# Layer 1's attention: two weight splits at its end instead of its start, and the compressed softmax's second half one turn later

## The chip, the cores and the metric

One core of a Trainium2 chip runs the whole program. TensorE (PE) multiplies, VectorE (DVE) and ScalarE (ACT) do elementwise work, GpSimd (POOL) scales the probabilities, and SyncE (SP) issues the weight loads. The metric is the device time of one execution, in microseconds (us), as the median of the executions timed; lower is better.

## The reference, cut to what matters

Two blocks follow each other; the change lies in layer 1 of the first. That layer's mixer has 16 heads in 4 groups of four and 256 queries, and adds up three attentions of each head: over 15 compressed keys, over selected keys and over a window. With 4 blocks of 64 keys all of them selected, and a window of 512 over 256 positions, the last two are plain causal attentions over different keys.

```python
s_c = jnp.einsum('bqgjd,bngd->bgjqn', qp, k_cmp).astype(jnp.float32) * scale
p_c = masked_softmax(s_c, cmp_end[None, :] <= qpos[:, None])
o_c = jnp.einsum('bgjqn,bngd->bqgjd', p_c.astype(v_cmp.dtype), v_cmp)
...
o = gc[..., 0:1] * o_c + gc[..., 1:2] * o_s + gc[..., 2:3] * o_w
...
return o.reshape(B, S, C_MIX_WIDTH) @ w_out
```

`masked_softmax` zeroes the masked places after the exponential and divides by the sum, at least 1e-20. A compressed key ends at position 31 or later, so the first 31 queries see none of them and get zeros. After the mixer come a product with `w_out` (1024 x 1024), the memory attention and the feed-forward.

## The kernel before

**Weights.** A weight matrix is cut into units of 128 x 2048 numbers (4 chunks of 128 rows by 512 columns). SP loads a unit into one of three slots `raw`; ACT writes its rounded copy `whi` (line 794, `hi`); DVE writes the rest, `wlo = raw - whi` (line 1250, `lo`); PE does three matmuls a chunk, with `whi`, `wlo` and `whi` (lines 2055 to 2057). A unit's load waits for the `lo` of the unit three before it, and its `hi` waits for the product that used that slot. Each engine has its own program, written out in order, and counts up semaphores for the others. `split_to(end)` splits the units up to `end` where it stands in ACT's program and in DVE's. The mixer's output product (`s["out"]`) has four units, here O0 to O3: O0 and O1 make the first 512 columns, O2 and O3 the second.

**The attention loop.** `attention` runs over 32 items (a head and a half of the queries, selected and window branch together), two of them a turn, `t = 0, 2, ..., 36`. In turn t, PE computes the scores of items t and t+1 (line 2146), which waits until DVE has masked the items before them; then runs `between(t)`; transposes the probabilities of items t-4 and t-3 (line 2156); and multiplies those of t-6 and t-5 with the values (lines 2163 and 2171, "PV" below). DVE takes the sums' reciprocals (1398, 1401), masks the scores with the causal bias and takes each row's minimum (1409), copies item t-4's transposed probabilities out of PSUM (1418), runs `between(t)` and `between(t+1)`, and every fourth turn writes a quarter of the product's input (`alo`, 1426). ACT takes exponentials (861), copies item t-3's transposed probabilities (871), runs `between(t)` and writes `ahi` (877). The last two turns only transpose and multiply; the output product begins as soon as PE has done the last PV. Turns alternate between scores 128 and 256 columns wide.

**The compressed softmax.** Its scores lie in four PSUM banks, two for each half `c` of the queries. Before the loop DVE adds the bias (1797), takes the maximum (1803) and subtracts it (1804), for both halves one after the other; ACT takes the exponentials (1133). In turns 0 and 2 of the loop (`compressed(1)` and `compressed(3)`) DVE multiplies a half by the mask `cmp_keep` (1815), sums (1816), bounds the sum from below (1817), inverts, multiplies by the gate and normalises (1818 to 1821). PE transposes both halves in turn 2 (2378); ACT copies the first, and DVE the second (1349), at the end of its turn 2. DVE and ACT split O0 in turn 6 and O1 in turn 10; O2 and O3 come after the loop.

Of the kernel before, what the change touches and what calls it, by code (L numbers as in the profile page):

```python
# [52 lines left out]
TINY = 1e-20  # L53
# [179 lines left out]
def build(nc, a, out):  # L233
    ctx = ExitStack()
    with ctx:
# [30 lines left out]
        cmp_bias, cmp_keep = sb("cmp_bias", [P, C, 32]), sb("cmp_keep", [P, C, 32])  # L266
# [423 lines left out]
        def _(pool):  # L690
# [15 lines left out]
            for c in range(C):  # L706
                step(pool.affine_select(out=cmp_keep[:, c, :], in_=cmp_keep[:, c, :], compare_op=ALU.is_ge, fill=0.0,
                                        base=P * c - (CMP_LEN - 1), pattern=[[-CMP_STRIDE, 32]], channel_multiplier=1))
# [77 lines left out]
        def _(act):  # L786
# [263 lines left out]
            for l in range(2):  # L1050
# [48 lines left out]
                else:  # L1099
# [31 lines left out]
                    for c in range(C):  # L1131
                        act.wait_ge(flag("cmp_shifted"), c + 1)
                        act.activation(CP[c], CS[c], ACT.Exp).then_inc(flag("cmp_exp"), 1)

                    def compressed(t):

                        if t == 0:
                            for b in range(2):
                                turn_copy(s["qrturn2"] + b, feat[:, 3072 + 512 * b:3584 + 512 * b])
                        if t == 2:  # L1140
                            turn_copy(s["cmpturn"], CPT[0])
                        if t in (6, 10):
                            split_to(s["vg"][-1].end + (t - 2) // 4)
# [100 lines left out]
        def _(dve):  # L1244
# [145 lines left out]
            def attention(items, run, banks, apart=False, between=None):  # L1390

                n, per = run.n, run.per
                for t in range(0, n + 6, 2):
                    for i in (t, t + 1):
# [8 lines left out]
                        if i < n:  # L1403
# [7 lines left out]
                            ins.then_inc(item_masked, 1)  # L1411
                    if 0 <= t - 4 < n:
# [244 lines left out]
            for l in range(2):  # L1657
# [88 lines left out]
                else:  # L1746
# [45 lines left out]
                    for c in range(C):  # L1792
# [14 lines left out]

                    def compressed(t):

                        if t in (1, 3):  # L1810
                            c = t // 2
                            cp4 = by_head(CP[c])
                            keep = cmp_keep[:, c, :].unsqueeze(1).broadcast_to([P, 16, 32])
                            dve.wait_ge(flag("cmp_exp"), c + 1)
                            step(dve.tensor_tensor(cp4, cp4, keep, ALU.mult))
                            step(dve.tensor_reduce(s_t[:, 0:16], cp4, AX, ALU.add))
                            step(dve.tensor_scalar(s_t[:, 0:16], s_t[:, 0:16], TINY, None, ALU.max))
                            step(dve.reciprocal(s_u[:, 0:16], s_t[:, 0:16]))
                            gate = GATE[:, c, :].rearrange("p (h b) -> p h b", b=3)[:, :, 0]
                            step(dve.tensor_tensor(s_u[:, 0:16], s_u[:, 0:16], gate, ALU.mult))  # L1820
                            dve.tensor_tensor(cp4, cp4, s_u[:, 0:16].unsqueeze(2).broadcast_to([P, 16, 32]), ALU.mult
                                              ).then_inc(flag("cmp_prob"), 1)
                        if t == 3:
                            turns(s["cmpturn2"], 1, lambda b: CPT[1])
                        if t in (6, 10):
                            split_to(s["vg"][-1].end + (t - 2) // 4)

                    attention(items1(), s["heads"], (2, 3, 0, 1), True, between=compressed)
# [223 lines left out]
        def _(pe):  # L2052
# [222 lines left out]
            for l in range(2):  # L2275
# [30 lines left out]
                else:  # L2306
# [61 lines left out]
                    def compressed(t):  # L2368
# [4 lines left out]
                        if t == 2:  # L2373
                            for c in range(C):
                                pe.wait_ge(flag("cmp_prob"), c + 1)
                                bank = turn_free(s["cmpturn"] + c)
                                for g in range(4):
                                    ins = pe.transpose(bank[:, P * g:P * g + P], CP[c][:, P * g:P * g + P], ident[:, :])
                                ins.then_inc(turned, 1)
# [240 lines left out]
```

## Time and profile before

| | |
|---|---|
| time, median of 3 runs | 1529.01 us (1528.53 to 1535.76) |
| the profiled execution: its time, its span | 1528.64 us, 1526.9 us |
| PE busy, of the span | 1371.0 us, 90% |
| DVE busy | 1053.4 us, 69% |
| ACT busy | 753.8 us, 49% |
| granted TensorE clock, mean of the span | 0.951 of full speed |

The span is what the trace covers; the time has 1.7 us more around it. Busy shares are means over the whole program. The loop of this change takes from 544 to 621 us of it, where the shares are others.

### The profile page before, as it was taken

How to read it: one execution, taken by the hardware profiler on the slowest of the kernel's cores; microseconds unless marked ns; L12 is line 12 of the kernel's file. 1: busy time of each engine (PE TensorE's matmuls, PEld its weight loads, DVE VectorE, ACT ScalarE, POOL GpSimd, SP SyncE). 2: the span in 40 equal slices, each digit the busy share in tenths (PEclk: the TensorE clock that was granted, in tenths of full speed). 3: DMA queues.
4: the chain of work that ended last, by engine and by line, in shares of the span. 5: the costliest groups of instructions: out<-in, count | busy, mean ns of one | idle time of the engine just before them, and what ended most of it. 6: DMA issues, size and time to landing. Idle time of an engine off the chain costs nothing.

```text
span 1526.9 us, 18368 instructions
## 1 busy us (share of the span) xinstructions
PE 1371.0 (90%) x6769; PEld 1130.9 (74%) x6769; DVE 1053.4 (69%) x1685; ACT 753.8 (49%) x943; POOL 110.1 (7%) x206
## 2 busy tenths in 40 slices
PE   6779698999998978889999998978789999999995
PEld 4667477788877856777888777867678787878784
DVE  4785766655554776676555478776567979888895
ACT  4343544444434446345444342553356757576773
POOL 0000301000000325120000000600000000000000
PEclk9989699999999979999999999999789999999997
DMA  6444024565546400234556634436548988989790
GB/s 226 141 164 138 15 70 138 166 192 191 176 157 164 137 18 32 64 128 159 188 192 192 186 126 150 162 114 212 207 151 302 337 323 313 346 283 354 284 348 28
DMA packets 123511, 277.63 MB, mean 182 GB/s; under 512 B 15383, under 2 KB 68781, under 8 KB 108077
## 3 DMA queue, kind: packets, MB, share of 16 engines
q1 hardware_dynamic: 121168, 275.99, 52.7%
q8 instruction: 46, 0.75, 0.2%
q10 hardware_dynamic: 2268, 0.65, 0.2%
q14 instruction: 29, 0.23, 0.0%
HBM read 275.57 MB, written 1.05 MB: 181 GB/s over the span
## 4 chain that ended last, share of the span: by engine, by line
PE 76%; DVE 15%; ACT 6%; issue 3%; ACTq 0%; POOL 0%; DVEq 0%
PE bank L2055 22%; PE bank L2057 21%; PE bank L2056 21%; PE bank L2490 2%; DVE t_wlo L1250 2%; DVE t_wlo L1261 2%; ACT t_whi L807 1%; PE bank L2156 1%; PE bank L2129 1%; PE bank L2146 1%; ACT t_whi L794 1%; DVE t_z L1409 1%; PE bank L2120 1%; PE bank L2171 1%; PE bank L2235 1%
## 5 line engine op out<-in xcount | busy, mean ns | idle before, releaser
L1250 DVE TENSOR_TENSOR t_wlo<-t_raw,t_whi 128x2048 fp32r<-128x2048 f32 (+3 forms) x144 | 316.6, 2209 | 151.2 <-ACT t_whi L794 150.0
L2055 PE MATMUL bank<-t_whi,t_ahi 128*128 128x512 f32 (+3 forms) x832 | 330.7, 397 | 31.2 <-DVE t_wlo L1250 13.2
L794 ACT ACTIVATE t_whi<-t_raw 128x2048 fp32r<-128x2048 f32 (+3 forms) x144 | 263.4, 1840 | 145.9 <-PE bank L2057 129.7
L2055 PE MATMUL bank<-t_whi,t_bhi 128*128 128x512 f32 (+1 forms) x800 | 314.3, 393 | 21.6 <-DVE t_z L1944 6.5
L2056 PE MATMUL bank<-t_wlo,t_ahi 128*128 128x512 f32 (+3 forms) x832 | 325.2, 391 | 0.0
L2057 PE MATMUL bank<-t_whi,t_alo 128*128 128x512 f32 (+3 forms) x832 | 325.1, 391 | 0.0
L2057 PE MATMUL bank<-t_whi,t_blo 128*128 128x512 f32 (+1 forms) x800 | 308.0, 385 | 0.0
L2056 PE MATMUL bank<-t_wlo,t_bhi 128*128 128x512 f32 (+1 forms) x800 | 307.7, 385 | 0.0
L2055 PEld LDWEIGHTS bank<-t_whi,t_ahi 128*128 128x128 f32 x832 | 159.4, 192 | 70.2 <-issue 28.3
L2055 PEld LDWEIGHTS bank<-t_whi,t_bhi 128*128 128x128 f32 x800 | 152.5, 191 | 53.6 <-issue 19.1
L2057 PEld LDWEIGHTS bank<-t_whi,t_alo 128*128 128x128 f32 x832 | 159.1, 191 | 32.2
L2056 PEld LDWEIGHTS bank<-t_wlo,t_ahi 128*128 128x128 f32 x832 | 159.4, 192 | 30.3
L2057 PEld LDWEIGHTS bank<-t_whi,t_blo 128*128 128x128 f32 x800 | 152.1, 190 | 30.5
L2056 PEld LDWEIGHTS bank<-t_wlo,t_bhi 128*128 128x128 f32 x800 | 152.6, 191 | 28.0
L1261 DVE TENSOR_TENSOR t_wlo<-t_raw,t_whi 128x2048 fp32r<-128x2048 f32 x51 | 116.2, 2288 | 26.4 <-ACT t_whi L807 26.1
L807 ACT ACTIVATE t_whi<-t_raw 128x2048 fp32r<-128x2048 f32 x51 | 97.9, 1920 | 40.4 <-PE bank L2057 40.3
L1261 DVE TENSOR_TENSOR t_wlo<-t_memo,t_whi 128x2048 fp32r<-128x2048 f32 x35 | 79.8, 2288 | 23.5 <-ACT t_whi L807 23.3
L807 ACT ACTIVATE t_whi<-t_memo 128x2048 fp32r<-128x2048 f32 x35 | 67.1, 1919 | 29.8 <-PE bank L2057 27.0
L1261 DVE TENSOR_TENSOR t_wlo<-t_feat,t_whi 128x2048 fp32r<-128x2048 f32 x34 | 77.6, 2287 | 4.9 <-ACT t_whi L807 4.7
L807 ACT ACTIVATE t_whi<-t_feat 128x2048 fp32r<-128x2048 f32 x34 | 65.2, 1919 | 25.3 <-PE bank L2057 25.1
L910 ACT ACTIVATE t_shared<-bank,t_half_scale 128x256 f32<-128x256 f32 x44 | 18.4, 470 | 76.8 <-PE bank L2057 73.5
L825 ACT ACTIVATE t_bhi<-bank,t_cols 128x256 fp32r<-128x256 f32 x40 | 15.7, 474 | 67.8 <-PE bank L2120 67.8
(370 smaller groups left out, 1421.7 us busy)
## 6 DMA issues: line engine op xcount, KB each, us to landing
t_raw<-in_ffn_w_in SPq DMA_DIRECT2D x88, 512.0 KB, 4.7
t_raw<-in_ffn_w_out SPq DMA_DIRECT2D x22, 1024.0 KB, 4.9
t_raw<-in_w_in SPq DMA_DIRECT2D x18, 1024.0 KB, 5.1
t_raw<-in_exp_w_up SPq DMA_DIRECT2D x18, 1024.0 KB, 6.9
t_raw<-in_exp_w_down SPq DMA_DIRECT2D x18, 1024.0 KB, 6.7
t_raw<-in_exp_w_gate SPq DMA_DIRECT2D x15, 1024.0 KB, 6.5
t_memo<-in_exp_w_gate SPq DMA_DIRECT2D x13, 1024.0 KB, 7.0
t_feat<-in_exp_w_up SPq DMA_DIRECT2D x13, 1024.0 KB, 7.1
```

The lines of the kernel that those rows point to most:

```text
L794: act.activation(whi[slot][:, 0:n], raw[slot][:, 0:n], ACT.Copy).then_inc(hi_done, 1)
L807: act.activation(whi[u % RING][:, :], RAW[slot], ACT.Copy).then_inc(hi_done, 1)
L825: ins = act.activation(dst[:, k, :], bank[:, T * n:T * n + T], ACT.Copy, scale=gain(k) if callable(gain) else gain)
L910: act.activation(silu[:, c, 0, :], TB[c][:, 0:FB], ACT.Tanh, scale=half_scale[:, c:c + 1]).then_inc(ff_tanh, 1)
L1250: dve.tensor_tensor(wlo[slot][:, 0:n], raw[slot][:, 0:n], whi[slot][:, 0:n].bitcast(F32), ALU.subtract).then_inc(lo_done, 1)
L1261: dve.tensor_tensor(wlo[u % RING][:, :], RAW[plan.raw_slot(u)], whi[u % RING][:, :].bitcast(F32), ALU.subtract).then_inc(lo_done, 1)
L1409: ins = dve.tensor_tensor_reduce(run.masked[g % 2][:, s_], SCB[g % 2][:, s_], b_.bias, -it.scale, -TAKEN, ALU.add, ALU.min, item_min[:, 2 ...
L2055: pe.matmul(dst, lhi, rhi_, start=start, stop=False)
L2056: pe.matmul(dst, lhi, rlo_, start=False, stop=False)
L2057: return pe.matmul(dst, llo, rhi_, start=False, stop=stop)
L2120: ins = pe.transpose(bank[:, T * n + P * c:T * n + P * c + P], src(c, 2 * b + n), ident[:, :])
L2490: ins = pe.matmul(y_bank(g, k // 4)[:, P * (k % 4):P * (k % 4) + P], x[:, c, k:D:KC], PICK[g % 2][:, c, :], start=c == 0, stop=c == 1)
```

## The change

Four edits, all in layer 1's attention:

1. O0 and O1 are split in turns 32 and 34 of the loop instead of turns 6 and 10, on ACT and DVE alike.
2. The second half's bias, maximum and subtraction move on DVE from ahead of the loop into turn 0, behind the masks of items 0 and 1; ACT's exponential of it moves into turn 0 too.
3. PE transposes the second half in turn 4 instead of turn 2, and DVE copies it in turn 4, ahead of item 0's copy (the new argument `ahead`).
4. The product with the mask and the lower bound of the sum go. `cmp_keep` shrinks to one number a row (0 for the 31 rows that see no compressed key, else 1), which goes in with the gate's product. The masked places carry a bias of -1e30 already, so their exponentials are zero wherever a row has a key.

```diff
-                    for c in range(C):
+                    def compressed_exp(c):
                         act.wait_ge(flag("cmp_shifted"), c + 1)
                         act.activation(CP[c], CS[c], ACT.Exp).then_inc(flag("cmp_exp"), 1)
+                    compressed_exp(0)
                     def compressed(t):
                         if t == 0:
+                            compressed_exp(1)
                             for b in range(2):
                                 turn_copy(s["qrturn2"] + b, feat[:, 3072 + 512 * b:3584 + 512 * b])
                         if t == 2:
                             turn_copy(s["cmpturn"], CPT[0])
-                        if t in (6, 10):
-                            split_to(s["vg"][-1].end + (t - 2) // 4)
+                        if t in (32, 34):
+                            split_to(s["vg"][-1].end + (t - 30) // 2)
...
+                    if ahead:
+                        ahead(t)
                     if 0 <= t - 4 < n:
                         i = t - 4
                         dve.wait_ge(turned, run.batch + i + 1)
...
+                    def compressed_prob(c):
+                        cp4 = by_head(CP[c])
+                        dve.wait_ge(flag("cmp_exp"), c + 1)
+                        step(dve.tensor_reduce(s_t[:, 0:16], cp4, AX, ALU.add))
+                        step(dve.reciprocal(s_u[:, 0:16], s_t[:, 0:16]))
+                        gate = GATE[:, c, :].rearrange("p (h b) -> p h b", b=3)[:, :, 0]
+                        step(dve.scalar_tensor_tensor(out=s_u[:, 0:16], in0=s_u[:, 0:16], scalar=cmp_keep[:, c, 0:1], in1=gate,
+                                                      op0=ALU.mult, op1=ALU.mult))
+                        dve.tensor_tensor(cp4, cp4, s_u[:, 0:16].unsqueeze(2).broadcast_to([P, 16, 32]), ALU.mult
+                                          ).then_inc(flag("cmp_prob"), 1)
+                    compressed_max(0)
                     def compressed(t):
+                        if t == 0:
+                            compressed_max(1)
                         if t in (1, 3):
-                            c = t // 2
-                            cp4 = by_head(CP[c])
-                            keep = cmp_keep[:, c, :].unsqueeze(1).broadcast_to([P, 16, 32])
-                            dve.wait_ge(flag("cmp_exp"), c + 1)
-                            step(dve.tensor_tensor(cp4, cp4, keep, ALU.mult))
-                            step(dve.tensor_reduce(s_t[:, 0:16], cp4, AX, ALU.add))
-                            step(dve.tensor_scalar(s_t[:, 0:16], s_t[:, 0:16], TINY, None, ALU.max))
...
-                        if t == 3:
-                            turns(s["cmpturn2"], 1, lambda b: CPT[1])
-                        if t in (6, 10):
-                            split_to(s["vg"][-1].end + (t - 2) // 4)
+                            compressed_prob(t // 2)
+                        if t in (33, 35):
+                            split_to(s["vg"][-1].end + (t - 31) // 2)
+                    def second_turn(t):
+                        if t == 4:
+                            turns(s["cmpturn2"], 1, lambda b: CPT[1])
...
-                        if t == 2:
-                            for c in range(C):
-                                pe.wait_ge(flag("cmp_prob"), c + 1)
...
+                        if t in (2, 4):
+                            c = t // 2 - 1
+                            pe.wait_ge(flag("cmp_prob"), c + 1)
```

**The start of the loop on DVE.** In the kernel before, from the second half's bias to the end of the first half's normalisation (the `ISA` rows are the masks of items 0 and 1; six more of them are left out):

```order
L1797 SCALAR_TENSOR_TENSOR t_shared<-bank,t_cmp_bias 128x128 x4
L1803 TENSOR_REDUCE t_s_t<-t_shared 128x16
L1804 TENSOR_TENSOR t_shared<-t_shared,t_s_t 128x512
L1409 ISA t_z,t_item_min<-bank,t_causal 128x128
L1409 ISA t_item_min 128x1
...
L1815 TENSOR_TENSOR t_z<-t_z,t_cmp_keep 128x512
L1816 TENSOR_REDUCE t_s_t<-t_z 128x16
L1817 TENSOR_SCALAR t_s_t<-t_s_t 128x16
L1818 RECIPROCAL t_s_u<-t_s_t 128x16
L1820 TENSOR_TENSOR t_s_u<-t_s_u,t_z 128x16
L1821 TENSOR_TENSOR t_z<-t_z,t_s_u 128x512
```

and in the changed kernel the same stretch:

```order
L1412 ISA t_z,t_item_min<-bank,t_causal 128x128
L1412 ISA t_item_min 128x1
...
L1803 SCALAR_TENSOR_TENSOR t_shared<-bank,t_cmp_bias 128x128 x4
L1809 TENSOR_REDUCE t_s_t<-t_shared 128x16
L1810 TENSOR_TENSOR t_shared<-t_shared,t_s_t 128x512
L1818 TENSOR_REDUCE t_s_t<-t_z 128x16
L1819 RECIPROCAL t_s_u<-t_s_t 128x16
L1821 SCALAR_TENSOR_TENSOR t_s_u<-t_s_u,t_cmp_keep,t_z 128x16
L1823 TENSOR_TENSOR t_z<-t_z,t_s_u 128x512
```

The masks of items 0 and 1 now stand ahead of the second half's three steps, and two of the six steps behind them are gone.

**The start of the loop on PE.** In the kernel before, from the scores of items 2 and 3 (256 wide) on; `t_ident<-t_z` rows are transposes of the compressed probabilities, `t_ident,t_feat` those of items 0 and 1:

```order
L2146 MATMUL bank<-t_feat 128x256 x2
L2146 MATMUL bank<-t_z,t_feat 128x256 x2
L2378 MATMUL bank<-t_ident,t_z 128x128 x8
L2146 MATMUL bank<-t_feat 128x128 x2
L2146 MATMUL bank<-t_z,t_feat 128x128 x2
L2156 MATMUL bank<-t_ident,t_feat 128x128 x4
```

and in the changed kernel:

```order
L2160 MATMUL bank<-t_feat 128x256 x2
L2160 MATMUL bank<-t_z,t_feat 128x256 x2
L2392 MATMUL bank<-t_ident,t_z 128x128 x4
L2160 MATMUL bank<-t_feat 128x128 x2
L2160 MATMUL bank<-t_z,t_feat 128x128 x2
L2392 MATMUL bank<-t_ident,t_z 128x128 x4
L2170 MATMUL bank<-t_ident,t_feat 128x128 x4
```

The scores of items 4 and 5 have moved ahead of the second half's transposes.

**The end of the loop on DVE.** In the kernel before, from the last reciprocals to O2's and O3's splits (`t_wlo`):

```order
L1398 RECIPROCAL t_item_inv<-t_item_sum 128x2
L1401 TENSOR_TENSOR t_item_inv<-t_item_inv,t_z 128x2
L1418 COPY t_shared<-bank 128x256
L1418 COPY t_shared<-bank 128x512
L1426 TENSOR_TENSOR t_alo<-bank,t_ahi 128x2x256
L1250 TENSOR_TENSOR t_wlo<-t_raw,t_whi 128x2048 x2
```

and in the changed kernel:

```order
L1401 RECIPROCAL t_item_inv<-t_item_sum 128x2
L1404 TENSOR_TENSOR t_item_inv<-t_item_inv,t_z 128x2
L1423 COPY t_shared<-bank 128x256
L1253 TENSOR_TENSOR t_wlo<-t_raw,t_whi 128x2048
L1423 COPY t_shared<-bank 128x512
L1253 TENSOR_TENSOR t_wlo<-t_raw,t_whi 128x2048
L1431 TENSOR_TENSOR t_alo<-bank,t_ahi 128x2x256
L1253 TENSOR_TENSOR t_wlo<-t_raw,t_whi 128x2048 x2
```

O0's split now stands between the copies of items 28 and 30, and O1's between the copy of item 30 and the last `alo`; on ACT the two `hi` stand behind the copies of items 29 and 31 in the same way.

## Rows read from the trace of the kernel before

**Rows 1.** Busy time and granted clock (PEclk) of seven stretches

```profile
core 0: us, PE busy (x) PEld busy (x) DVE busy (x) ACT busy (x) POOL busy (x), PEclk, DMA share, GB/s
161.00:183.00 22.00, 15.97 (x88) 11.19 (x90) 19.31 (x91) 9.25 (x37) 8.01 (x18) 0.51 0.01 2
279.00:286.00 7.00, 4.56 (x23) 3.49 (x22) 6.11 (x8) 5.05 (x5) 0.00 (x0) 1.00 0.51 150
547.00:556.00 9.00, 3.65 (x14) 2.35 (x15) 8.07 (x33) 5.68 (x20) 1.51 (x4) 0.50 0.00 0
556.00:571.00 15.00, 10.86 (x76) 7.85 (x74) 9.21 (x39) 6.93 (x22) 4.68 (x10) 0.70 0.02 1
621.00:650.00 29.00, 28.08 (x149) 23.86 (x147) 19.40 (x35) 12.64 (x19) 0.00 (x0) 1.00 0.28 87
917.00:920.00 3.00, 0.47 (x5) 0.50 (x6) 2.43 (x2) 0.00 (x0) 0.00 (x0) 1.00 0.13 38
920.00:923.50 3.50, 3.50 (x13) 2.93 (x12) 2.96 (x6) 0.00 (x0) 0.00 (x0) 0.51 0.85 292
```

**Rows 2.** Timeline of PE in the loop: start, duration, line, tiles, idle before

```profile
555.54 1.12 PE L2378 MATMUL bank<-t_ident,t_z 128*128 128x128 f32 x4 [3.66 <-DVE t_z L1821]
...
559.54 1.23 PE L2146 MATMUL bank<-t_feat 64*128 64x256 f32 x4 [0.67 <-DVE t_item_min L1409]
...
564.92 0.51 PE L2146 MATMUL bank<-t_feat 64*128 64x128 f32 x4
...
571.30 0.75 PE L2146 MATMUL bank<-t_feat 64*128 64x256 f32 x4 [3.50 <-DVE t_item_min L1409]
...
582.18 1.22 PE L2146 MATMUL bank<-t_feat 64*128 64x256 f32 x4 [3.54 <-DVE t_item_min L1409]
...
586.62 0.49 PE L2146 MATMUL bank<-t_feat 64*128 64x128 f32 x4
...
599.79 0.49 PE L2146 MATMUL bank<-t_feat 64*128 64x128 f32 x4 [0.80 <-DVE t_item_min L1409]
```

**Rows 3.** Timeline of DVE in turns 0 to 6 of the loop

```profile
544.79 0.88 DVE L1797 SCALAR_TENSOR_TENSOR t_shared<-bank,t_cmp_bias 128x128 f32<-128x128 f32 x4
...
547.03 0.28 DVE L1409 CUSTOM_DVE_ANT_0 t_z<-bank,t_causal 128x128 f32<-128x128 f32 x1
...
547.87 0.69 DVE L1815 TENSOR_TENSOR t_z<-t_z,t_cmp_keep 128x512 f32<-128x512 f32 x1
...
549.31 0.17 DVE L1817 TENSOR_SCALAR t_s_t<-t_s_t 128x16 f32<-128x16 f32 x1
...
550.63 0.16 DVE L1398 RECIPROCAL t_item_inv<-t_item_sum 128x2 f32<-128x2 f32 x1
...
552.55 0.78 DVE L1815 TENSOR_TENSOR t_z<-t_z,t_cmp_keep 128x512 f32<-128x512 f32 x1
...
556.70 0.69 DVE L1349 COPY t_shared<-bank 128x512 f32<-128x512 f32 x1 [1.21 <-PE bank L2378]
...
567.56 2.29 DVE L1250 TENSOR_TENSOR t_wlo<-t_raw,t_whi 128x2048 fp32r<-128x2048 f32 x1 [1.77 <-ACT t_whi L794]
```

**Rows 4.** Timeline of ACT: O0's `hi`, turn 32's copy, O3's `hi`

```profile
565.62 1.90 ACT L794 ACTIVATE t_whi<-t_raw 128x2048 fp32r<-128x2048 f32 x1
...
616.48 0.38 ACT L871 ACTIVATE t_shared<-bank 128x256 f32<-128x256 f32 x1 [1.88 <-PE bank L2171]
...
626.90 1.92 ACT L794 ACTIVATE t_whi<-t_raw 128x2048 fp32r<-128x2048 f32 x1 [2.37 <-PE bank L2057]
```

**Rows 5.** Timeline of the loop's end: DVE's last copy, PE's last PV, the output product

```profile
618.99 0.69 DVE L1418 COPY t_shared<-bank 128x512 f32<-128x512 f32 x1 [2.12 <-PE bank L2171]
...
619.83 0.44 PE L2163 MATMUL bank<-t_shared,t_z 128*64 128x128 f32 x4 [0.94 <-DVE t_shared L1418]
...
621.07 0.50 PE L2055 MATMUL bank<-t_whi,t_ahi 128*128 128x512 f32 x1
```

**Rows 6.** Loads issued from 560 to 660 us: KB each, median us to landing

```profile
t_raw<-in_nsa_w_out SPq DMA_DIRECT2D x1, 1024.0 KB, 5.1
```

More of the change, by code:

```diff
@@ L52 @@
 TAKEN = -3e38
-TINY = 1e-20
 ROPE_THETA = 500000.0
@@ L265, in build @@
         zero = sb("zero", [P, T])
-        cmp_bias, cmp_keep = sb("cmp_bias", [P, C, 32]), sb("cmp_keep", [P, C, 32])
+        cmp_bias, cmp_keep = sb("cmp_bias", [P, C, 32]), sb("cmp_keep", [P, C, 1])
         shared = sb("shared", [P, 2600])
@@ L707, in _ @@
                 step(pool.affine_select(out=cmp_keep[:, c, :], in_=cmp_keep[:, c, :], compare_op=ALU.is_ge, fill=0.0,
[L708 removed]
+                                        base=P * c - (CMP_LEN - 1), pattern=[[-CMP_STRIDE, 1]], channel_multiplier=1))
             for t in range(16):
@@ L1388, in rope, with attention @@
                 step(dve.tensor_tensor(v2, t[2], t[3], ALU.add))
-            def attention(items, run, banks, apart=False, between=None):
+            def attention(items, run, banks, apart=False, between=None, ahead=None):
                 n, per = run.n, run.per
@@ L1790, in by_head, with compressed_max @@
                         return b_.rearrange("p (h n) -> p h n", h=16)
-                    for c in range(C):
+                    def compressed_max(c):
                         dve.wait_ge(flag("cmp_scored"), c + 1)
@@ L1816, in compressed @@
-                            step(dve.tensor_reduce(s_t[:, 0:16], cp4, AX, ALU.add))
-                            step(dve.tensor_scalar(s_t[:, 0:16], s_t[:, 0:16], TINY, None, ALU.max))
[L1818 to L1822, printed above, removed]
@@ L1823, in compressed @@
-                        if t == 3:
+                            compressed_prob(t // 2)
[3 more added lines that the diff above has]
+                        if t == 4:
                             turns(s["cmpturn2"], 1, lambda b: CPT[1])
-                        if t in (6, 10):
-                            split_to(s["vg"][-1].end + (t - 2) // 4)
-                    attention(items1(), s["heads"], (2, 3, 0, 1), True, between=compressed)
+                    attention(items1(), s["heads"], (2, 3, 0, 1), True, between=compressed, ahead=second_turn)
@@ L2372, in compressed @@
                             turns(s["qrturn2"], JOBSQ[4:8], drain=False)
-                        if t == 2:
-                            for c in range(C):
-                                pe.wait_ge(flag("cmp_prob"), c + 1)
[L2376 to L2379, printed above, removed]
+                        if t in (2, 4):
+                            c = t // 2 - 1
+                            pe.wait_ge(flag("cmp_prob"), c + 1)
+                            bank = turn_free(s["cmpturn"] + c)
+                            for g in range(4):
+                                ins = pe.transpose(bank[:, P * g:P * g + P], CP[c][:, P * g:P * g + P], ident[:, :])
+                            ins.then_inc(turned, 1)
                     pe.wait_ge(flag("cmp_read"), 1)
```

## The prediction

> **What bounds the kernel now.** The page's busy line says only that PE leads over the whole program, so a change pays where PE waits. To find out where it does, I took stretches of time. Behind this loop, from 621 to 650 us, PE is busy 28.08 of 29 us at the full granted clock [rows 1]: nothing that DVE or ACT is spared there can help. Inside the loop it is otherwise: PE is busy 3.65 of 9 us from 547 to 556 us and 10.86 of 15 us from 556 to 571 us, at granted clocks of 0.50 and 0.70, so mostly at 1.2 GHz instead of 2.4 [rows 1]. Last I followed PE's own timeline through the loop for what ended each wait. There are three large ones: 3.66 us until DVE had normalised the second compressed half, 3.50 us and 3.54 us until DVE had masked the next items [rows 2]. The reader is to see that the second and third stand right behind the two splits: DVE waits 1.77 us for O0's `hi`, then works 2.29 us on `wlo`, and the masks queue behind both [rows 3]. O1's split in turn 10 does the same ahead of 582.18. In the span of this loop DVE's order sets PE's pace.
>
> **Part 1: no splits in turns 6 and 10.** I price this by like with like. From turn 8's scores to turn 16's, PE takes 586.62 - 564.92 = 21.70 us, with both stalls in it. From turn 16's scores to turn 24's, the same kinds of turns and also one `alo` among them, without a split, it takes 599.79 - 586.62 = 13.17 us [rows 2]. The difference, 8.53 us, is what the two splits cost together with the clock that fell behind each wait. It can't be more than twice the whole path through DVE (1.90 of `hi` and 2.29 of `wlo`, so 8.4 us for two) plus the lost clock, and not less than the two waits beyond what is left in a quiet turn (0.80 us at 599.79): 3.50 + 3.54 - 1.6 = 5.4 us [rows 2 to 4]. I take 8.5, since the second measure is of these same turns in the steady state that they would be in. The one condition is that turn 8 starts at the full clock, as the first did nearly; if it doesn't, below.
>
> **Part 2: turns 0 to 6.** Followed along DVE from 544.79 us, when the scores of items 0 and 1 are there [rows 3]:
> - The two items' masks, 0.84 us (547.87 - 547.03), now come first: to 545.6.
> - The second half's bias, maximum and subtraction, 2.24 us (547.03 - 544.79): to 547.9.
> - The first half's normalisation was 2.76 us (550.63 - 547.87). Without the mask's product (0.69) and the bound (0.17) it is 1.9; the gate's product stays one small instruction, for which I take the same time as before: to 549.8.
> - Turn 2's reciprocals and masks, 1.92 us (552.55 - 550.63): to 551.7. PE may then score items 4 and 5, which stood behind the second half's transposes before.
> - The second half's normalisation, 1.9 us: to 553.6. PE transposes it, 1.12 us [rows 2]: to 554.8. DVE masks items 4 and 5 meanwhile. That turn has no row among those shown; from 0.84 us for its masks and under 1.92 for a turn with wider ones I take 1.4: to 555.0.
> - DVE copies the second half, 0.7 us: to 555.7. This copy is the new wait: item 1's transposes need the bank that it empties. They take half of 1.12 us: to 556.4 with the semaphore's way. Then PE can score items 6 and 7, which it did at 559.54.
>
> So turn 6 starts 3.1 us earlier. Bounds: of this 1.7 us is arithmetic taken out (twice 0.86), and that holds if the reordering brings nothing; at most the whole 3.66 us wait goes plus 0.9. From turn 6 to turn 8 nothing changes (5.38 us, 564.92 - 559.54), at the low clock. ACT's exponential of the second half waits for 547.9 and lies beside DVE's normalisation of the first; the two copies behind it on ACT are first read in turn 16. The smaller `cmp_keep` is made in the first microseconds and costs nothing.
>
> **Part 3: the splits at the end.** ACT's copy in turn 32 starts at 616.48 and takes 0.38; O0's `hi` follows, and its `wlo` begins some 1.9 us later as it did (567.56 - 565.62), then takes 2.29: to 621.1 on the old time axis [rows 3, 4]. Queued behind it on DVE is the copy of item 30, which started at 618.99 [rows 5]. It is 2.1 us late, and with it the last PV (619.83), for which PE has nothing else to do. The loop's end moves from 621.07 to 623.2 on that axis. O1's `hi` stands behind item 31's copy on ACT, which comes when item 30's did, and ends at about 621.5; its `wlo` begins behind DVE's late copy, at 621.8, and ends at 624.1, with the last `alo` queued behind it. PE needs both only after O0's product, 5.8 us past the loop's end (O3's `hi`, which waits for that product, starts at 626.90) [rows 4, 5]. That hides them; with the cover gone O1's split would cost up to its 2.3 us. If the splits fell wholly into waits, this part would be free; if all of both `hi` and `wlo` lay on the path, 8.4 us. I take 2.1.
>
> Loads: O3's load waits for O0's `wlo`, so its issue moves from 570 us to 2 us before the loop's end. It takes 5.1 us [rows 6] and lands 3.1 us past the end; its `hi` can't start before 5.8. The memory query weights behind it in SP's queue wait for O1's `wlo`, 0.9 us past the end, and are used only behind the whole output product.
>
> **The clock in the tail.** PE's wait ahead of the last PV grows from 0.94 us [rows 5] to 3.0. In the stretch from 917 to 920 us PE is busy only 0.47 of 3 us, and the next 3.5 us run at 0.51; in the stretch from 279 to 286 us it is idle 2.44 of 7 us and the clock stays at 1.00 [rows 1]. A wait of 3 us lies nearer the first. At 1.2 GHz for 3.5 us, dense product work loses 1.7 us. Either can happen, so I put in the middle, 0.8 us, and both ends into the range. The Trainium skill ("TensorE: Matmul & The Clock Gate", section "HAM oscillation — how this bites in real kernels") speaks against this edit: a burst of matmuls behind a long enough wait starts at half rate, every time the wait comes, and loses half of the throttled time. By it, with this wait taken for long enough, the sum is -7.8 us; if the clock doesn't react, it is -9.5. This trace shows both: a fall at 920 us (0.51), none at 279 us (1.00).
>
> **The sum.** -8.5 - 3.1 + 2.1 + 0.8 = -8.7 us. Made against the profiled execution's own 1528.64 us, which lies 0.4 under the median of 1529.01: about 1519.9 us.
>
> **The rivals.**
> - *The tail eats it* (no change to be told, 0.19). O0's and O1's splits both lie on the path to the end, and the output product starts at the low clock: 2.1 + 2.3 + 1.7 = 6.1 us against 11.6 gained, 1523.1 us. For it: nothing else runs in the last turns to absorb them. Against it: O1's `wlo` is not needed for 5.8 us.
> - *The low clock lasts* (slower, 0.04). PE stays at 1.2 GHz through the loop. Layer 0's attention did from 161 to 183 us, at 0.51, where PE was busy 15.97 of 22 us [rows 1]. A turn took 5.38 us at the low clock, against 3.3 as the mean of the four quiet ones (13.17 / 4), so each turn loses 2.1. Twelve turns with scores are left from turn 8 on: 25.2 - 8.7 = 16.5 us slower, 1545.1. It decides from the fifth such turn on. Against it: the clock rose while turn 6 ran without a large wait, which is what the change makes more of.
> - *The start gains nothing by order* (0.10, within the forecast's sign). The new copy ahead of item 0's holds up PE as long as the old wait did; only the 1.7 us of arithmetic are saved: 1521.3.
> - *More than forecast* (0.12). The clock rises a turn or two earlier than it did, since PE has fewer holes from 547 us on, and the tail keeps its clock: another 2.1 + 0.8 us, 1517.0.
> - The forecast itself has 0.55.
>
> **How the numbers follow.** Half a per cent, 7.6 us, is about what a measurement of this kernel can tell from no change. The forecast, the fourth and most of the third lie beyond it: faster 0.75, same 0.21, slower 0.04. The range runs from the fourth rival with some room (1515.7) to a little past the first (1523.8).
>
> **What the profile after would show.** No `wlo` between turns 6 and 12, and no wait of PE over 1.5 us from there to turn 30; four turns at about 13.2 us from turn 8 on. Turn 6's scores 3.1 us sooner behind turn 0's. One wait of about 3 us ahead of the last PV, released by DVE's copy, with O0's `wlo` right in front of it. The output product as long as before or, with the clock down, 1.7 us longer. The prediction is wrong if turns stay longer than 3.3 us without a split, if PE waits for O0 or O1 once the product runs, or if the clock falls in the middle of the loop with no wait ahead of it.

## The result, and the profile after

The changed kernel takes 1520.88 us (median of 5 runs, 1517.49 to 1523.11). The kernel before took 1532.84 us beside it (5 runs, 1528.53 to 1535.76). The ratio is 0.9924, 95% interval 0.9897 to 0.9950: faster by 0.8%. Measured again, with 12 runs against 35, it is 1521.46 us and 0.9936 [0.9913, 0.9959]. Forecast were 1519.9 us, 8.7 us under the kernel before, and a range of 1515.7 to 1523.8. The time lies in the range. The difference is 12.0 us by the medians of the first measurement and 8.4 us by those of the second.

The profiled execution took 1521.83 us. The page of its profile says, of the span and of each engine's busy time, share and instructions:

```profile
span 1520.0 us, 18364 instructions
...
PE 1372.4 (90%) x6769; PEld 1133.0 (75%) x6769; DVE 1050.2 (69%) x1681; ACT 754.5 (50%) x943; POOL 110.4 (7%) x206
```

PE does the same work in a span 6.9 us shorter; DVE has lost 3.2 us of work. The gain is in the waits. Windows of the changed kernel, with the columns of [rows 1]; the first two are stretches of [rows 1]:

```profile
547.00:556.00 9.00, 5.21 (x30) 3.85 (x29) 8.59 (x37) 5.46 (x20) 2.20 (x6) 0.69 0.00 0
556.00:571.00 15.00, 13.60 (x115) 9.76 (x115) 9.81 (x57) 10.05 (x41) 8.44 (x18) 0.80 0.00 1
605.00:613.00 8.00, 4.48 (x47) 3.56 (x43) 5.51 (x4) 4.58 (x4) 0.16 (x1) 0.81 0.24 63
613.00:617.00 4.00, 4.00 (x12) 3.19 (x11) 1.22 (x2) 3.34 (x3) 0.00 (x0) 0.53 0.74 269
617.00:630.00 13.00, 13.00 (x59) 10.77 (x58) 7.82 (x13) 1.92 (x1) 0.00 (x0) 1.00 0.24 81
```

At the loop's start PE is now busy 5.21 of 9 us and 13.60 of 15, where it was 3.65 and 10.86. At its end there is a hole, and the output product runs at the low clock (0.53) until about 617 us.

PE's timeline in the changed kernel (start, duration, line, tiles, idle before), as in [rows 2] and [rows 5]:

```profile
551.22 0.66 PE L2392 MATMUL bank<-t_ident,t_z 128*128 128x128 f32 x4 [1.88 <-DVE t_z L1823]
...
555.02 1.12 PE L2392 MATMUL bank<-t_ident,t_z 128*128 128x128 f32 x4 [0.66 <-DVE t_z L1823]
...
557.71 1.22 PE L2160 MATMUL bank<-t_feat 64*128 64x256 f32 x4
...
562.66 0.49 PE L2160 MATMUL bank<-t_feat 64*128 64x128 f32 x4
...
575.46 0.49 PE L2160 MATMUL bank<-t_feat 64*128 64x128 f32 x4 [0.80 <-DVE t_item_min L1412]
...
588.70 0.49 PE L2160 MATMUL bank<-t_feat 64*128 64x128 f32 x4 [0.80 <-DVE t_item_min L1412]
...
610.66 0.69 PE L2177 MATMUL bank<-t_shared,t_z 128*64 128x128 f32 x4 [2.85 <-DVE t_shared L1423]
...
612.99 0.80 PE L2069 MATMUL bank<-t_whi,t_ahi 128*128 128x512 f32 x1
```

The three waits of 3.5 us and more are gone. Turns 8 to 16 take 575.46 - 562.66 = 12.80 us instead of 21.70. One wait of 2.85 us has come ahead of the last PV (610.66), where there was one of 0.94. What stands before it shows on DVE, whose timeline at the loop's end is (compare [rows 5]):

```profile
605.37 0.42 DVE L1423 COPY t_shared<-bank 128x256 f32<-128x256 f32 x1 [1.91 <-PE bank L2185]
607.62 2.29 DVE L1253 TENSOR_TENSOR t_wlo<-t_raw,t_whi 128x2048 fp32r<-128x2048 f32 x1 [1.83 <-ACT t_whi L793]
609.83 0.68 DVE L1423 COPY t_shared<-bank 128x512 f32<-128x512 f32 x1
610.43 2.28 DVE L1253 TENSOR_TENSOR t_wlo<-t_raw,t_whi 128x2048 fp32r<-128x2048 f32 x1
```

DVE waits 1.83 us for O0's `hi`, subtracts for 2.29 us, and only then copies item 30's probabilities, for which PE waits.

To add it all up I cut the loop at landmarks, from DVE's first row of the compressed bias to PE's first transposes behind the loop, within the output product. In us:

| stretch | before | after | difference |
|---|---|---|---|
| first bias to turn 6's scores | 17.00 | 14.22 | -2.78 |
| turn 6's scores to turn 8's | 5.38 | 4.95 | -0.43 |
| turn 8's to turn 16's | 21.70 | 12.80 | -8.90 |
| turn 16's to turn 30's | 22.64 | 22.71 | +0.07 |
| turn 30's to the loop's end | 11.81 | 14.82 | +3.01 |
| product, to PE's next transposes | 16.46 | 18.19 | +1.73 |
| this part of the program | 94.99 | 87.69 | -7.30 |
| all the rest of the span | 1431.9 | 1432.3 | +0.4 |

This explains the 6.9 us between the two spans. The medians differ by more, 12.0 and 8.4 us; the experiments on the kernel before tell where part of that comes from.

### The profile page after: what moved, and what is told of

Read it like the earlier page. It is cut to its first block, busy times and chain, and to the rows that moved or that the text cites. A ratio compares the mean times of both kernels' runs of the same rounds, so it can differ in the third digit from the quotient of the medians.

```text
span 1520.0 us, 18364 instructions
## 1 busy us (share of the span) xinstructions
PE 1372.4 (90%) x6769; PEld 1133.0 (75%) x6769; DVE 1050.2 (69%) x1681; ACT 754.5 (50%) x943; POOL 110.4 (7%) x206
## 4 chain that ended last, share of the span: by engine, by line
PE 74%; DVE 14%; ACT 5%; issue 3%; DMA 2%; ACTq 1%; POOL 0%; DVEq 0%; SPq 0%
PE bank L2069 21%; PE bank L2070 20%; PE bank L2071 20%; PE bank L2504 2%; DVE t_wlo L1264 2%; DVE t_wlo L1253 2%; DMA t_raw<-in_ab_w_in 2%; ACT t_whi L806 1%; PE bank L2143 1%; PE bank L2185 1%; PE bank L2170 1%; DVE t_z L1412 1%; PE bank L2160 1%; ACT t_whi L793 1%; PE bank L2134 1%
```

## The experiments

Beside the two kernels there are eight variants. Ratios are to the kernel before, timed on the same chip. "Local" is the part of the table above: 94.99 us in the profiled execution of before, 87.69 us in that of the changed kernel.

**1. The changed kernel again** (`after_again`).

> The changed kernel once more, to have it timed beside the parts. The theory (splits out of the turns -8.9 us, start of the loop -2.8 us, the split in front of the last copy +1.9, the clock's fall in the tail +0 to +2.8) gives -7 to -9.8 us on the kernel before, a ratio of 0.9936 to 0.9954. The rival, that the times say more than one profile does and that some of the gain lies outside the loop, gives -11 us or more, a ratio under 0.993.

1521.46 us, 0.9936 [0.9913, 0.9959]. Local 87.71 us, each landmark within 0.03 us of the first profile, the last PV's wait again 2.85 us. So what the profile says of this loop repeats. The ratio is at the edge of the 0.9936 to 0.9954 expected.

**2. Only the splits moved** (`splits_at_end_only`): the kernel before with edit 1.

```diff
-                        if t in (6, 10):
-                            split_to(s["vg"][-1].end + (t - 2) // 4)
+                        if t in (32, 34):
+                            split_to(s["vg"][-1].end + (t - 30) // 2)
```

and on DVE `(33, 35)` in the same way.

> Only edit 1: O0 and O1 split in turns 32 and 34, the start of the loop as before. The theory: -8.9 + 1.9 us and 0 to 2.8 us for the clock in the tail, so -4.2 to -7.0 us; PE takes 12.8 to 13.2 us from turn 8's scores to turn 16's, and waits about 2.9 us ahead of the last PV. The rival, that these turns run at the full clock only because the start of the loop leaves PE fewer holes: turns 8 to 16 take 15 us or more and the gain is under 4 us.

1524.4 us, 0.9952 [0.9932, 0.9972]. PE's timeline:

```profile
558.70 1.11 PE L2378 MATMUL bank<-t_ident,t_z 128*128 128x128 f32 x4 [3.65 <-DVE t_z L1821]
...
567.99 0.49 PE L2146 MATMUL bank<-t_feat 64*128 64x128 f32 x4
...
580.78 0.49 PE L2146 MATMUL bank<-t_feat 64*128 64x128 f32 x4 [0.80 <-DVE t_item_min L1409]
```

The wait at the start is still there (3.65 us, before 3.66), and turn 6's scores come at 17.00 us, counted from DVE's first bias, as before. Turns 8 to 16 take 580.78 - 567.99 = 12.79 us all the same. The gain of part 1 needs nothing of the new start. Local is 89.38 us.

At the loop's end O0's `wlo` stands ahead of the copy as in the changed kernel, and PE waits the same 2.85 us:

```profile
617.32 0.44 PE L2163 MATMUL bank<-t_shared,t_z 128*64 128x128 f32 x4 [2.85 <-DVE t_shared L1418]
...
618.57 0.50 PE L2055 MATMUL bank<-t_whi,t_ahi 128*128 128x512 f32 x1
```

Yet the clock does not fall behind this wait. It was low before it, as PE's windows show:

```profile
608.00:613.00 5.00, 3.76 (x28) 0.66 0.00 0
613.00:625.00 12.00, 9.15 (x67) 1.00 0.41 132
```

The product's stretch takes 16.50 us, as in the kernel before, and turn 30 to the loop's end 15.07 us. So the wait of 2.85 us alone does not settle what the clock does. By ratio the gain is 7.3 us, a little over the 7.0 that was the upper end of what was expected.

**3. Only the start changed** (`start_only`): the changed kernel with the splits back in turns 6 and 10.

```diff
-                        if t in (32, 34):
-                            split_to(s["vg"][-1].end + (t - 30) // 2)
+                        if t in (6, 10):
+                            split_to(s["vg"][-1].end + (t - 2) // 4)
```

> Only edits 2 to 4: the splits stay in turns 6 and 10. The theory: -2.8 to -3.2 us, all of it ahead of turn 6's scores; the two waits of 3.5 us stay, and the loop's end looks as before. The rival: the splits' waits take the gain back, since O0's split comes at its own pace, and the time is the same within 1 us.

1528.54 us, 0.9977 [0.9957, 0.9998]. PE's timeline:

```profile
566.49 1.02 PE L2160 MATMUL bank<-t_feat 64*128 64x256 f32 x4 [3.50 <-DVE t_item_min L1412]
...
577.65 1.23 PE L2160 MATMUL bank<-t_feat 64*128 64x256 f32 x4 [3.77 <-DVE t_item_min L1412]
```

Both waits are back and turns 8 to 16 take 22.92 us. Turn 6's scores come at 13.92 us, 3.08 us sooner than in the kernel before: part 2 alone. The last PV waits 0.94 us again, so the 2.85 us belong to the splits. (Even so the clock was low from 611.1 to 617.9 us, and turn 30 to the loop's end takes 14.45 us, so that local is 95.34 us, no less than the 94.99 of the first profile of before; experiment 9 is about that.) In ratios, -0.48% of experiment 2 and -0.23% of this one make -0.71%, against -0.64% for the whole change: the two parts add up, within the intervals.

**4. Only the shorter arithmetic** (`no_mask_only`): the kernel before with edit 4, in the old order. `cmp_keep` stays 32 wide, and its first column is used.

```diff
-                            step(dve.tensor_tensor(cp4, cp4, keep, ALU.mult))
...
-                            step(dve.tensor_scalar(s_t[:, 0:16], s_t[:, 0:16], TINY, None, ALU.max))
...
-                            step(dve.tensor_tensor(s_u[:, 0:16], s_u[:, 0:16], gate, ALU.mult))
+                            step(dve.scalar_tensor_tensor(out=s_u[:, 0:16], in0=s_u[:, 0:16], scalar=cmp_keep[:, c, 0:1], in1=gate,
+                                                          op0=ALU.mult, op1=ALU.mult))
```

> Only edit 4: the product with the mask and the lower bound of the sum are gone, every step stands where it stood before. The theory has 0.93 us of DVE's time per half on the path, so turn 6's scores come 1.9 us sooner and the time falls by 1.9 us; the rest of the start's 2.8 us belongs to the order. The rival, that DVE's arithmetic is what counts and the order nothing: turn 6's scores come 2.8 us sooner here too.

1527.4 us, 0.9972 [0.9951, 0.9993]. Turn 6's scores come at 15.87 us, 1.13 us sooner, not the 1.7 of part 2's lower bound, nor the 1.9 expected. This execution is no clean comparison: TensorE's clock fell at 541.4 us, 0.3 us behind DVE's first bias (in the profile of before it was 2.0 us), and DVE waited 0.53 us for the second half's compressed scores, as its timeline shows:

```profile
541.15 0.89 DVE L1797 SCALAR_TENSOR_TENSOR t_shared<-bank,t_cmp_bias 128x128 f32<-128x128 f32 x4 [1.81 <-PE bank L2362]
...
544.01 0.89 DVE L1797 SCALAR_TENSOR_TENSOR t_shared<-bank,t_cmp_bias 128x128 f32<-128x128 f32 x4 [0.53 <-PE bank L2362]
```

The second half's bias came 2.86 us behind the first's, where it took 2.25 in the kernel before (544.79 [rows 3] less 542.54, its first row). That is 0.61 us, and 1.13 + 0.61 makes the 1.7. The kernel before bears this out: in the first of the profiles of experiment 9 the two biases lie 2.56 us apart, 0.31 more than 2.25, and turn 6's scores come 0.31 us later, at 17.31. The times can't tell edit 4 alone (0.9972) from all of the start (0.9977); only the landmarks do, 1.13 against 3.08 us.

**5. The first split behind the last copy** (`o0_behind_last_copy`): the changed kernel, where DVE does O0's `lo` behind item 30's copy, and O1's behind the last `alo`.

```diff
-                        if t in (33, 35):
-                            split_to(s["vg"][-1].end + (t - 31) // 2)
+                        if t == 35:
+                            split_to(s["vg"][-1].end + 1)
```

> The changed kernel with O0's wlo behind DVE's copy of item 30 and O1's behind the last alo; the hi stay in turns 32 and 34. The theory: the copy is in time again, PE's wait ahead of the last PV is 0.94 us instead of 2.85, and the output product waits some 0.9 us for O0's wlo instead: 1.0 us better than the changed kernel by that alone, and up to 2.8 us more where the clock stays up. A ratio of 0.991 to 0.993. The rival, that the clock falls in the tail whatever the last wait is: only the 1.0 us, a ratio of 0.993.

1520.1 us, 0.9911 [0.9880, 0.9942]. PE's timeline:

```profile
608.43 0.44 PE L2177 MATMUL bank<-t_shared,t_z 128*64 128x128 f32 x4 [0.94 <-DVE t_shared L1423]
...
610.74 0.47 PE L2069 MATMUL bank<-t_whi,t_ahi 128*128 128x512 f32 x1 [1.00 <-DVE t_wlo L1253]
```

The last PV's wait is 0.94 us again, and the product waits 1.00 us for O0's `wlo`. The product's stretch takes 16.41 us instead of 18.19, since the clock is up. Local is 85.31 us, 2.4 under the changed kernel, although the clock was low in the last turns, from 601.7 to 605.1 us. The long wait is therefore the work of O0's `wlo` ahead of the copy, and the split can be had for less. In the times the two can't be told apart.

**6. The tail kept busy** (`tail_kept_busy`): the changed kernel, with 12 matmuls more ahead of the last PV, whose result nobody reads. They stand in place of the wait.

```diff
+                        if n == 32 and t == n + 4:
+                            pe.wait_ge(item_masked, run.first + n)
+                            for _ in range(12):
+                                pe.matmul(SCB[0][:, :], ahi[:, 1, 0:P], bhi[:, 0:2, :].rearrange("p k t -> p (k t)"), start=True, stop=True)
```

> The changed kernel with 12 matmuls of 512 columns, whose result nobody reads, in PE's wait ahead of the last PV (2.7 us at the full clock). Nothing waits for them but the last PV behind them on PE. The theory, that this wait brings the clock down: it stays at 1.00, the last PV and the output product take 16.5 us and not 18.2, and the time is 2 to 2.8 us under the changed kernel's, a ratio of 0.9918 to 0.9925. The rival, that the fall comes from the two turns ahead of the wait: the clock falls all the same, and the time is as the changed kernel's or up to 1 us longer.

1521.88 us, 0.9920 [0.9889, 0.9951]. Windows, with the columns of [rows 1]:

```profile
604.00:612.40 8.40, 7.63 (x74) 6.01 (x74) 4.71 (x4) 4.60 (x5) 1.65 (x3) 1.00 0.10 9
612.40:620.00 7.60, 7.60 (x35) 6.30 (x34) 3.78 (x3) 5.09 (x4) 0.00 (x0) 1.00 0.60 211
```

The clock stays at 1.00 through the end of the loop and into the product, and local falls from 87.69 to 84.90 us. The dependencies are the same, and `wlo` still stands ahead of the copy. So 2.8 us is what the low clock cost in the tail. This is one execution, and experiment 2 shows that the clock can stay up even with the wait left empty. The time doesn't show the 2.8 us: 0.9920 can't be told from the changed kernel's 0.9936, and outside this part the profiled execution took 1435.5 us against 1432.3.

**7. Halves of the splits in the loop's small waits** (`halves_in_waits`): the changed kernel, with four `hi` halves of 128 x 1024 on ACT in turns 16, 20, 24 and 28, and four `lo` halves on DVE in turns 20, 24, 28 and 32, ahead of the copy. Only the calls are shown.

```diff
-                        if t in (32, 34):
-                            split_to(s["vg"][-1].end + (t - 30) // 2)
+                        if t in (16, 20, 24, 28):
+                            hi_half(s["vg"][-1].end + (t - 16) // 8, t // 4 % 2)
...
-                        if t in (33, 35):
-                            split_to(s["vg"][-1].end + (t - 31) // 2)
+                        if t in (20, 24, 28, 32):
+                            lo_half(s["vg"][-1].end + (t - 20) // 8, (t // 4 + 1) % 2)
```

> The changed kernel with O0 and O1 split in halves of 1024 columns: ACT's in turns 16, 20, 24 and 28, DVE's in turns 20, 24, 28 and 32, each ahead of the copy, where DVE waits 1.1 to 1.9 us for PE. The theory, that a split costs only where it is longer than the wait it stands in: turns 16 to 30 take 22.7 us as before plus at most 0.5, the last PV's wait is 0.94 us, and 1.9 us of the tail come back, with up to 2.8 of the clock's: a ratio of 0.9905 to 0.9925. The rival, that any split in the loop delays the masks or PE: each half costs 1.2 us, turns 16 to 30 take 26 us or more, and the ratio is 0.994 or above.

1523.24 us, 0.9933 [0.9905, 0.9961]. DVE's timeline:

```profile
581.89 1.29 DVE L1275 TENSOR_TENSOR t_wlo<-t_raw,t_whi 128x1024 fp32r<-128x1024 f32 x1
583.20 0.42 DVE L1442 COPY t_shared<-bank 128x256 f32<-128x256 f32 x1
...
590.18 1.43 DVE L1275 TENSOR_TENSOR t_wlo<-t_raw,t_whi 128x1024 fp32r<-128x1024 f32 x1
```

DVE waits some 1.2 us at these places in a quiet turn; the halves take 1.29 and 1.43 us and make the copy behind them late. Turns 16 to 30 take 24.51 us instead of 22.71, more than the 0.5 us expected on top, and PE's longest wait there is 1.75 us, with the clock low behind it from 587.9 to 591.1 us. At the end 14.82 fall to 14.04 us and the product runs at the full clock. Local is 87.02 us: the splits' place in the middle costs 1.8 us and spares about 2.5, so nothing is decided between them. The ratio of 0.9933 is worse than the 0.9905 to 0.9925 expected.

**8. The second half's maximum ahead of the loop** (`second_max_ahead`): the changed kernel with that step in its old place.

```diff
                     compressed_max(0)
+                    compressed_max(1)
...
-                        if t == 0:
-                            compressed_max(1)
```

> The changed kernel with the second half's bias, maximum and subtraction ahead of the loop again; the other edits stay. The theory has DVE's work on the path in either order, and in the changed order DVE waited 0.29 us for the first scores: turn 6's scores come 0.3 to 0.5 us sooner than in the changed kernel (13.7 to 13.9 us behind the first bias, not 14.2), and the time can't be told from the changed kernel's. The rival, that the first masks' place ahead is what brings the gain of the start: turn 6's scores come 1 us later or more.

1522.16 us, 0.9917 [0.9884, 0.9949]. Turn 6's scores come at 13.83 us against 14.22. In the changed kernel DVE, with the masks first, waits 0.29 us for their scores, as its timeline shows:

```profile
543.49 0.88 DVE L1803 SCALAR_TENSOR_TENSOR t_shared<-bank,t_cmp_bias 128x128 f32<-128x128 f32 x4 [1.81 <-PE bank L2378]
...
546.11 0.29 DVE L1412 CUSTOM_DVE_ANT_0 t_z<-bank,t_causal 128x128 f32<-128x128 f32 x1 [0.29 <-PE bank L2160]
...
546.96 0.88 DVE L1803 SCALAR_TENSOR_TENSOR t_shared<-bank,t_cmp_bias 128x128 f32<-128x128 f32 x4
```

How much of the 0.39 us is the order is less clear. With the masks first, turn 6's scores come at 13.91 to 14.25 us in six profiles (experiments 1, 3, 5, 6, 7 and the changed kernel's own), and in experiment 10, with the maximum ahead, at 14.16. Turn 8's scores repeat better: 19.17 or 19.18 us behind the first bias in those six, 18.97 here and 18.73 in experiment 10. So the new place of this step is worth nothing and seems to cost 0.2 to 0.4 us; local is 87.58 us, the same.

**9. Where the kernel before varies** (`before_look1`, `before_look2`, `before_look3`): the kernel before, profiled three times more.

> The kernel before, profiled once more. Its times lie in two heaps, near 1528 and near 1535 us, and the profile read for the prediction is of the lower. The theory, that the clock's falls come at other moments from one execution to the next: an execution near 1535 us shows more or longer stretches at 1.2 GHz, inside this loop or outside it, with the same instructions. The rival, that something else (a load, a wait at the start) makes the 7 us: the clock's stretches are alike and one stretch of the program is longer.

> The same again, since one execution in two or so is of the upper heap: more or longer stretches at 1.2 GHz by the theory, one longer stretch of the program with a like clock by the rival.

> A third look at the kernel before: more or longer stretches at 1.2 GHz by the theory, one longer stretch of the program with a like clock by the rival.

These executions took 1528.42, 1533.27 and 1536.08 us. Local is 95.80, 98.40 and 98.42 us. The first keeps the clock at the loop's end, as its windows show (PE's columns alone: length, busy, clock, DMA share, GB/s):

```profile
615.00:625.00 10.00, 7.82 (x76) 1.00 0.01 2
...
700.00:720.00 20.00, 17.57 (x80) 1.00 0.48 159
935.00:950.00 15.00, 14.60 (x73) 1.00 0.65 212
```

and the third doesn't:

```profile
615.00:625.00 10.00, 6.92 (x51) 0.66 0.00 0
...
700.00:720.00 20.00, 17.57 (x76) 0.91 0.52 176
935.00:950.00 15.00, 12.89 (x55) 0.89 0.63 211
```

though its last waits are as short as ever; its PE timeline:

```profile
620.28 1.94 PE L2156 MATMUL bank<-t_ident,t_feat 128*128 128x128 f32 x8 [0.67 <-DVE t_shared L1418]
...
624.64 0.44 PE L2163 MATMUL bank<-t_shared,t_z 128*64 128x128 f32 x4 [0.94 <-DVE t_shared L1418]
```

From turn 30's scores to the loop's end it takes 14.44 us instead of 11.82, so 2.6 us for the clock alone; the second execution does the same (14.40 us). The turns with the splits vary too. From turn 8 to turn 16 the three take 22.84, 22.86 and 22.88 us, and experiments 3 and 4, whose splits stand there as well, 22.92 and 23.01. The 21.70 us of the profile that the prediction was made from is the least of six. PE's waits in it are as long within 0.3 us (3.50 and 3.54 us, against 3.50 to 3.83 in the others), but a stretch at the low clock behind one of them is shorter: 571.8 to 575.2 us, against 570.9 to 577.8 in the first of the three.

The mean local of all four profiled executions of before is (94.99 + 95.80 + 98.40 + 98.42) / 4 = 96.90 us. Against 87.70 of the changed kernel that is -9.2 us. The ratio 0.9936 of 1529.87 us is -9.8, and the medians of that measurement differ by 8.4. The rest of the spread lies elsewhere: outside this part the third execution takes 1435.9 us against the first's 1430.8, with low clock near 715 and 943 us.

**10. Both improvements together** (`both_better`): the edits of experiments 5 and 8 in one kernel.

> The changed kernel with O0's wlo behind the copy of item 30, O1's behind the last alo, and the second half's maximum ahead of the loop: what the two earlier runs found better, together. The theory: from the first bias to the end of the output product's first six groups 84.9 us (87.7 in the changed kernel, 85.3 with the first alone), and a ratio of 0.990 to 0.9925. The rival: nothing beyond the first alone, since 0.3 us at the start is lost in waits behind it.

1519.84 us, 0.9942 [0.9923, 0.9962]. Its PE timeline has

```profile
609.00 0.44 PE L2176 MATMUL bank<-t_shared,t_z 128*64 128x128 f32 x4 [0.94 <-DVE t_shared L1423]
...
611.31 0.47 PE L2068 MATMUL bank<-t_whi,t_ahi 128*128 128x512 f32 x1 [0.99 <-DVE t_wlo L1253]
```

and local is 83.63 us, 4.1 under the changed kernel and the least of all. Of the 1.7 us that it lies under experiment 5, 1.3 are the clock, which stays up in the last turns here and didn't there (turn 30 to the loop's end takes 12.88 us, there 14.22); only 0.45 us, up to turn 8's scores, can belong to the added edit. The ratio missed the 0.990 to 0.9925 expected, and can't be told from the changed kernel's (0.9936). It beats the kernel before; whether it beats the changed one stays open.

## Why the prediction was right, step by step

**Part 1, no splits in turns 6 and 10: right.** Forecast -8.5 us, measured -8.90. Pricing by like with like held: a quiet stretch of four turns had taken 13.17 us, and these took 12.80. PE's longest wait from turn 6 to turn 30 is 0.80 us. Experiment 2 gives 12.79 without the new start. The condition set on turn 8's clock was not tested: it had risen just before turn 8's scores in both (562.1 us for 562.66, 567.8 for 567.99). The 21.70 us that the price started from was a good execution, though: the mean of four is 22.57, which makes -9.8 us.

**Part 2, turns 0 to 6: right in size, with two details off.** Forecast -3.1 us, measured -2.78 in the changed kernel and -3.08 in experiment 3. Up to turn 8's scores the two are alike, -3.21 and -3.20 us: what the changed kernel has less by turn 6 it has back in turn 6 (0.43 against 0.12 us). The step that put the masks at once behind 544.79 us left out that their scores can come later: DVE waits 0.29 us for them in the changed kernel. The gate's product takes a little more than the instruction in its place before, 0.24 against 0.18 us. DVE's copy of the second half, the new wait ahead of item 0's, takes 0.68 us, forecast 0.7. The DVE timeline of the changed kernel holds the steps:

```profile
549.20 0.68 DVE L1818 TENSOR_REDUCE t_s_t<-t_z 128x16 f32<-128x512 f32 x1
...
550.20 0.24 DVE L1821 SCALAR_TENSOR_TENSOR t_s_u<-t_s_u,t_cmp_keep,t_z 128x16 f32<-128x16 f32 x1
...
551.09 0.16 DVE L1401 RECIPROCAL t_item_inv<-t_item_sum 128x2 f32<-128x2 f32 x1
...
553.00 0.68 DVE L1818 TENSOR_REDUCE t_s_t<-t_z 128x16 f32<-128x512 f32 x1
...
556.29 0.68 DVE L1352 COPY t_shared<-bank 128x512 f32<-128x512 f32 x1
```

The first half's normalisation takes 551.09 - 549.20 = 1.89 us, forecast 1.9; turn 2's reciprocals and masks 553.00 - 551.09 = 1.91, forecast 1.92. The rival that the start gains nothing by order fell: 3.08 us against 1.13 for the arithmetic alone.

**Part 3, O0's split ahead of item 30's copy: right.** Forecast +2.1 us. From turn 32's copy to item 30's it is 609.83 - 605.37 = 4.46 us, before 618.99 - 616.45 = 2.54, so +1.92. PE's wait is 2.85 us, forecast 3.0. O1's split and the loads are hidden, as said: from 612.99 us the product runs without a wait, and ACT's timeline has O3's `hi` behind the product that frees its slot, not behind a load:

```profile
620.56 1.92 ACT L793 ACTIVATE t_whi<-t_raw 128x2048 fp32r<-128x2048 f32 x1 [4.11 <-PE bank L2071]
```

**The clock in the tail: the mis-sized term.** I put 0.8 us, with 0 and 1.7 as bounds; in the changed kernel it is 2.8, by the rows below and by experiment 6. I had counted the product alone. The clock is low from 609.9 to 616.8 us, and the last PV lies in that too: it takes 612.99 - 610.66 = 2.33 us instead of 621.07 - 619.83 = 1.24. Up to O3's `hi` the product then takes 620.56 - 612.99 = 7.57 us instead of 5.83. That makes 1.09 + 1.74 = 2.83. The second number is the 1.7 that I had as the upper bound. The case "nearer the first", for which the row at 917 us spoke, came in both profiles of the changed kernel. The other came too: in experiment 2, behind the same wait of 2.85 us, the product ran at the full clock, and in experiment 8 the clock fell only at 613.4 us, so that the last PV kept it (18.04 us for the product's stretch). The Trainium skill ("TensorE: Matmul & The Clock Gate", section "HAM oscillation — how this bites in real kernels") had it as a burst at half rate behind the wait. The trace agrees: 0.53 from 613 to 617 us. The trace of experiment 2 shows no such burst behind a wait as long: 1.00 from 613 to 625 us.

**Why the total is near all the same.** By the profiled pair the sum is -2.78 - 0.43 - 8.90 + 0.07 + 3.01 + 1.73 = -7.3 us, 1.4 less than the -8.7 forecast, and the tail's 2.0 us too little are the cause. But the kernel before pays 2.6 us in the same tail in two of its four profiled executions, and so do experiments 3 and 4, whose tail is the same (14.45 and 14.51 us from turn 30 on, against 11.8). Two of four, or four of six, is 1.3 to 1.7 us on average, which comes off what the low clock adds to the changed kernel. The turns with the splits add 0.9 more (22.57 less 21.70). So the means of the profiles differ by 9.2 us, on the other side of the forecast. These averages rest on few profiles and are estimates. What the times say of the difference, -8.4 us by the medians of the longer measurement, -9.8 by its ratio and -12.0 by the medians of the first, brackets the forecast only loosely. That 1520.88 us came within 1.0 us of 1519.9 is therefore partly luck: the forecast took 8.7 us off 1528.64, while the kernel before had a median of 1532.84 in that measurement, and two errors of about 1 and 2 us, the price of the splits and that of the clock, have opposite signs.

**The rivals.** The tail eats it: O1's split costs nothing, so no. The low clock lasts: no, the granted clock is 1.00 behind 617 us, and turns 16 to 30 take as long as before. More than forecast: turn 6 was shorter by 0.43 us, not by a whole turn's 2.1, and the tail lost its clock in both profiles.

## What to carry to other kernels

A weight split on an engine that paces a loop costs about twice the work of that engine (8.9 us here for two subtractions of 2.29), since the wait for ScalarE's half of the split and the fallen clock come on top, and it is paid in the loop's turns; look for a place behind the last thing that another engine waits for, not just ahead of it (experiment 5). When a change opens one wait of about 3 us ahead of dense work, price the low clock over the whole stretch, including the work between the wait and the dense part. It may not come: here it cost 2.8 us in two executions, 1.6 in a third and nothing in a fourth. Before comparing two profiles, profile each kernel several times: a single pair gave -7.3 us where the mean gives -9.2.

## What was not expected of the hardware

The same kernel, with the same waits at this loop's end (1.50, 0.67 and 0.94 us), lost its clock there in two executions of four, for 2.6 us each. Over all fourteen profiles the clock falls in the last turns, before PE's wait for the last PV, in eight, for 1.3 to 2.6 us where it can be priced. Behind the last PV's wait it is another matter. The four profiles in which PE stands idle there for 2.85 us are the changed kernel's two and those of experiments 2 and 8, and the clock falls in or just behind that wait in three of them. In the ten others, with a wait of 0.94 us or with matmuls in its place, the output product never runs at the low clock, and its stretch takes 16.4 to 16.5 us. Twelve matmuls that nobody reads, 3.0 us long, took the place of the wait and cost nothing to be seen, since PE had nothing else to do there; that they kept the clock up fits these counts and rests on one execution. What decides between the outcomes stays open.
